# Expert coefficients by accumulating scatters from GpSimd in place of one-hot matmuls

## The reference, cut to what matters

```python
top_s, top_i = lax.top_k(sc, PEER_TOPK)               # 16 of 128 keys, in both halves
cand_s = top_s[:, :, 0, :, None] + top_s[:, :, 1, None, :]
best_s, best_pos = lax.top_k(cand_s, PEER_TOPK)       # 16 of the 256 sums
idx = jnp.take_along_axis(cand_i, best_pos, axis=-1)  # expert = 128 * first + second
g = jax.nn.softmax(best_s, axis=-1)
act = gelu(einsum('phkd,pd->phk', expert_u[idx], xb))
return einsum('phk,phkd->pd', g * act, expert_v[idx])
```

## Time and profile before

| | us |
|---|---|
| median of 3 runs | 2823.46 (2823.13 to 2825.11) |
| profiled execution, whole | 2823.46 |
| its span | 2821.4 |
| PE busy | 2656.9 (94%) |
| VectorE busy | 1571.4 (56%) |
| ScalarE busy | 921.2 (33%) |
| GpSimd busy | 524.8 (19%) |

### The profile page before, as it was taken

How to read it: one execution, slowest core, us unless ns; L and a number is a source line. 1 busy time by engine, 2 the same in 40 slices (tenths; PEclk the granted TensorE clock), 3 DMA queues, 4 the chain that set the end, 5 groups by cost and what they waited for, 6 DMA issues and landing times.

```text
span 2821.4 us, 30879 instructions
## 1 busy us (share of the span) xinstructions
PE 2656.9 (94%) x11948; PEld 2161.4 (77%) x11948; DVE 1571.4 (56%) x2920; ACT 921.2 (33%) x1344; POOL 524.8 (19%) x308
## 2 busy tenths in 40 slices
PE   3989987989899999999999999999999998999998
PEld 2777876767678888888888888888778766888887
DVE  7864598897976344433344456555363456533432
ACT  4433332323233232222322332334342443322221
POOL 5424332222222000000000000003330443111100
PEclk9988999989999999999999999999999799999999
DMA  6533234434446332333323545443234013222232
GB/s 243 201 112 120 88 122 131 161 111 150 149 148 210 132 127 99 126 126 119 127 95 129 189 177 216 154 153 128 70 109 143 4 60 105 91 96 97 90 96 84
DMA packets 146088, 358.97 MB, mean 127 GB/s; under 512 B 9652, under 2 KB 75316, under 8 KB 140696
## 3 DMA queue, kind: packets, MB, share of 16 engines
q1 hardware_dynamic: 141272, 304.31, 32.2%
q0 software_dynamic: 4672, 52.69, 4.8%
HBM read 298.44 MB, written 56.62 MB: 126 GB/s over the span
## 4 chain that ended last, share of the span: by engine, by line
PE 66%; DVE 4%; ACT 1%; issue 1%; DMA 1%; SPq 0%; POOL 0%; ACTq 0%; DVEq 0%; POOLq 0%
PE bank L448 20%; PE bank L444 20%; PE bank L445 20%; PE bank L572 1%; PE bank L724 1%; DVE one_hot L1533 1%; DVE prob_lo L1269 1%; PE bank L726 1%; PE bank L725 1%; PE bank_stat L470 0%; ACT prob_hi L1084 0%; PE bank L694 0%; DMA weight<-expert_coefs 0%; DVE one_hot L1528 0%; PE bank L710 0%
## 5 line engine op out<-in xcount | busy, mean ns | idle before, releaser
L444 PE MATMUL bank<-h_lo,weights_hi 128*128 128x512 f32 x2176 | 882.3, 405 | 36.8 <-ACT weights_hi L792 31.6
L445 PE MATMUL bank<-h_hi,weights_hi 128*128 128x512 f32 x2176 | 870.9, 400 | 0.0
L792 ACT ACTIVATE weights_hi<-weights_raw 128x1024 fp32r<-128x1024 f32 (+1 forms) x411 | 430.8, 1049 | 484.0 <-PE bank L448 382.9
L448 PE MATMUL bank<-h_hi,weights_lo 128*128 128x512 f32 x2176 | 556.4, 396 | 5.3 <-DVE weights_lo L1227 5.3
L444 PEld LDWEIGHTS bank<-h_lo,weights_hi 128*128 128x128 f32 x2176 | 417.9, 192 | 141.2 <-ACT weights_hi L792 31.9
L445 PEld LDWEIGHTS bank<-h_hi,weights_hi 128*128 128x128 f32 x2176 | 417.4, 192 | 98.0 <-issue 0.2
L448 PEld LDWEIGHTS bank<-h_hi,weights_lo 128*128 128x128 f32 x2176 | 410.2, 189 | 106.0 <-DVE weights_lo L1227 6.2
L1859 POOL TENSOR_TENSOR weights_lo<-weights_raw,weights_hi 128x1024 fp32r<-128x1024 f32 x128 | 320.5, 2507 | 625.3 <-ACT weights_hi L792 625.3
L1227 DVE TENSOR_TENSOR weights_lo<-weights_raw,weights_hi 128x1024 fp32r<-128x1024 f32 (+1 forms) x283 | 359.1, 1271 | 35.2 <-ACT weights_hi L792 34.6
L1421 DVE SCALAR_TENSOR_TENSOR residual<-bank,ada,residual 128x512 f32<-128x512 f32 x136 | 102.3, 752 | 406.1 <-PE bank L448 406.0
L444 PE MATMUL bank<-mixed_lo,weights_hi 128*128 128x512 f32 x768 | 299.0, 389 | 0.0
(11 more groups left out here) (353 smaller groups left out, 2633.7 us busy)
## 6 DMA issues: line engine op xcount, KB each, us to landing
weights_raw<-in_expert_u SPq DMA_DIRECT2D x128, 512.0 KB, 3.5
weights_raw<-in_expert_v SPq DMA_DIRECT2D x128, 512.0 KB, 3.3
expert_coefs<-stage SPq DMA_DIRECT2D x32, 1024.0 KB, 6.3
weight<-expert_coefs POOLq DMA_DIRECT2D x16, 2048.0 KB, 8.7
ada_raw<-in_w_ada SPq DMA_DIRECT2D x40, 512.0 KB, 4.5
hidden_store<-hidden SPq DMA_DIRECT2D x14, 1024.0 KB, 5.8
hidden<-hidden_store POOLq DMA_DIRECT2D x7, 2048.0 KB, 14.8
weights_raw<-in_w_ffn_gate SPq DMA_DIRECT2D x22, 512.0 KB, 3.2
```

The source lines that it names most:

```text
L444: M.matmul(bank[:], hi[:, c:c + P], m_lo[k], start=start and i == 0, stop=False)
L445: M.matmul(bank[:], hi[:, c:c + P], m_hi[k], start=False, stop=False)
L448: ins = M.matmul(bank[:], lo[:, c:c + P], m_hi[k], start=False, stop=stop and i == len(tiles) - 1)
L792: S.activation(w_hi[n % SPLIT][:, 0:w], w_raw[n % RAW][:, 0:w], ACT.Copy).then_inc(*hi_done.inc(n))
```

## The change

Places are now found by addresses. After a set of 128 tokens is routed, VectorE works out for each token and each of its 128 choices the address of the coefficient in DRAM (`place`, three instructions), and the softmax weights stand in `share`. GpSimd issues 4 x 8 x 16 = 512 indirect transfers: each takes one column of share (one word of each of 128 partitions) and adds it at the 128 addresses in `expert_coefs` (L1843 of the changed kernel). It waits after each 16 until they have landed, since two heads may choose one expert. Before that SyncE writes zeros over the 33.5 MB of expert_coefs, in 64 stores of 512 KB placed among the loads of w_in, w_out, w_q and the first 36 blocks of expert_u. The layout in DRAM has the 128 tokens of a set as its innermost dimension, so that a group's coefficients come in four loads with rows of 512 bytes, where before it was one load with 16 KB for each partition.

AHEAD is 15: 120 blocks of expert_u come in a row, with nothing between them on PE. 14 groups of activations are stored and read back instead of 7. Group 14 of expert_v comes after blocks 120 to 127, then groups 15 and 0 to 13. Low parts of expert_u from block 2 on are made by VectorE. The second pair of tiles (h_hi/h_lo) serves every other group from group 0 on; groups 14 and 15 both use mixed_hi/mixed_lo. The set of 128 tokens number tb is routed one step a block: blocks 0 to 9, 10 to 27, 28 to 45 and 46 to 63.

```diff
-AHEAD = 8
+AHEAD = 15
 KEPT = AHEAD - 1
-FIRST_U = 8
-PLACE_U = (16, 16, 15, 9)
+ROUTE_STEPS = HEADS + HEADS // 2 + 4 + 2
...
-POOL_LOW = set(range(0, BLOCK_AT["expert_u", AHEAD * GROUP - 1] + 2)) \
+POOL_LOW = set(range(0, BLOCK_AT["expert_u", 2])) \
...
-            second = N_GROUPS - 1 - KEPT
-            PAIR[g] = (i - second + 1) % 2 if i >= second else 0
+            PAIR[g] = (i + 1) % 2 if i else 0
...
+        ROUTED_AT = [[None] * HEADS + list(range(ROUTE_STEPS - HEADS))]
+        for tb in range(1, TB):
+            ROUTED_AT.append([ROUTED_AT[-1][-1] + 1 + n for n in range(ROUTE_STEPS)])
...
-            for j in range(FIRST_U):
+            for j in range(AHEAD * GROUP):
                 hidden_product(j)
-            turn_chosen(0)
-            for tb, n, first, end in PLACING:
-                for quad in range(first, end):
-                    place(tb, quad)
-                if n == PLACE_U[tb] - 1 and tb + 1 < TB:
-                    turn_chosen(tb + 1)
-                hidden_product(placed_block(tb, n))
...
+            for j in range(AHEAD * GROUP):
+                for tb in range(TB):
+                    if ROUTED_AT[tb][-2] == j:
+                        soften(tb)
                 hidden_gelu(j)
...
-                    if not (KEPT <= g < N_GROUPS - 2):
+                    if i:
                         mix_hi(i + 1, k)
...
+                if i == 0:
+                    for n in range(GROUP):
+                        mix_hi(1, n)
...
+                chain(V.scalar_tensor_tensor(place_f[:], chosen[:, 1, :], float(N_KEYS), chosen[:, 0, :], ALU.mult, ALU.add))
+                chain(V.tensor_scalar(place_f[:], place_f[:], float(P), col("token"), ALU.mult, ALU.add))
+                chain(V.tensor_scalar(place[:, tb, :], place_f[:], float(tb * N_KEYS * N_KEYS * P), None, ALU.add))
...
+            for j in range(AHEAD * GROUP):
+                for tb in range(TB):
+                    if j in ROUTED_AT[tb]:
+                        next(routers[tb])
+                split_lo(BLOCK_AT["expert_u", j] + 2)
...
+                if i == 0:
+                    for n in range(GROUP):
+                        late.append((MIX_ORDER[1], n))
+                        finish_mix()
...
-            for j in range(AHEAD * GROUP):
-                split_lo(BLOCK_AT["expert_u", j] + 2)
+            split_lo(BLOCK_AT["expert_u", 2])
-            G.wait_ge(*stage_stored[0][T // TOK - 2])
-            G.wait_ge(*stage_stored[1][T // TOK - 1])
+            for tb in range(TB):
+                G.wait_ge(*zeros_stored[tb][TB * TB - 1])
+                G.wait_ge(*dve["routed", tb])
+                for h in range(HEADS):
+                    if h:
+                        G.wait_ge(*scattered[tb, h - 1, TOPK - 1])
+                    for n in range(TOPK):
+                        c = h * TOPK + n
+                        G.indirect_dma_start(out=coefs[:], out_offset=bass.IndirectOffsetOnAxis(ap=place[:, tb, c:c + 1], axis=0),
+                                             in_=share[:, tb, c:c + 1], in_offset=None, compute_op=ALU.add) \
+                            .then_inc(*scattered.inc((tb, h, n)))
+            G.wait_ge(*scattered[TB - 1, HEADS - 1, TOPK - 1])
...
-                    G.dma_start(weight[g % 2][:].rearrange("p s j t -> p (s j t)"),
-                                coefs[g].rearrange("p s j t -> p (s j t)")).then_inc(*weight_landed[g % 2].inc(g))
+                    for tb in range(TB):
+                        G.dma_start(weight[g % 2][:, :, tb * P:tb * P + P],
+                                    coefs_of[tb, g * GROUP:g * GROUP + GROUP].rearrange("j p t -> p j t")) \
+                            .then_inc(*weight_landed[g % 2].inc((g, tb)))
...
+            def store_zeros():
+                if zeroed[0] < TB * TB * TB:
+                    tb, n = divmod(zeroed[0], TB * TB)
+                    Y.dma_start(coefs_of[tb, GROUP * n:GROUP * n + GROUP].rearrange("j p t -> p j t"),
+                                zeros[:].unsqueeze(1).broadcast_to([P, GROUP, P])).then_inc(*zeros_stored[tb].inc(n))
+                    zeroed[0] += 1
```

More of the change, by code:

```diff
@@ L202, in build @@
         keys_landed = signal("keys_landed", 16)
-        stage_stored = [signal(f"stage{i}_stored", 16) for i in range(2)]
+        zeros_stored = [signal(f"zeros{tb}_stored", 16) for tb in range(TB)]
+        scattered = signal("scattered", 16)
         hidden_stored = [signal(f"hidden{i}_stored", 16) for i in range(2)]
@@ L558, in hidden_product @@
                 product(("u", j), BLOCK_AT["expert_u", j], h_hi_tiles, h_lo_tiles)
[L560 to L564, removed]
-                ins.then_inc(*pe.inc(("turn", tb)))
-            def place(tb, quad):
-                bank = take(("place", tb, quad))
-                M.wait_ge(*dve["hot", tb, quad])
-                hot = one_hot[quad % N_HOT]
-                for t in range(4):
-                    ins = M.matmul(bank[:, t * P:(t + 1) * P], hot[:, 0, t, :], hot[:, 1, t, :], start=True, stop=True)
-                ins.then_inc(*pe.inc(("place", tb, quad)))
-            for j in range(FIRST_U):
-                hidden_product(j)
-            turn_chosen(0)
-            for tb, n, first, end in PLACING:
-                for quad in range(first, end):
-                    place(tb, quad)
-                if n == PLACE_U[tb] - 1 and tb + 1 < TB:
-                    turn_chosen(tb + 1)
-                hidden_product(placed_block(tb, n))
+            for j in range(AHEAD * GROUP):
+                hidden_product(j)
             for i, g in enumerate(MIX_ORDER):
@@ L1029, in mix_hi @@
                         S.wait_ge(*pe["v", pair_over, KD - 1])
-                    if PAIR[g] and not PAIR[MIX_ORDER[i - 1]] and i > 1:
+                    if PAIR[g] and not PAIR[MIX_ORDER[i - 1]]:
                         S.wait_ge(*pe["u", N_KEYS - 1])
@@ L2021, in save_hidden @@
                         .then_inc(*hidden_stored[g % 2].inc((g, n)))
-            def store_stage(tb, quad):
-                s = (tb * P + 4 * quad) // TOK
-                Y.wait_ge(*act["place", tb, quad])
-                Y.dma_start(coefs[:, :, s, :, :].rearrange("g p j t -> p g (j t)"),
-                            stage[s % 2][:].rearrange("p g j t -> p g (j t)")).then_inc(*stage_stored[s % 2].inc(s))
-            for j in range(FIRST_U):
+            for j in range(AHEAD * GROUP):
                 load_weights(BLOCK_AT["expert_u", j] + 5)
                 save_hidden(j)
-            for tb, n, first, end in PLACING:
-                for quad in range(first, end):
-                    if 4 * quad % TOK == TOK - 4:
-                        store_stage(tb, quad)
-                j = placed_block(tb, n)
-                load_weights(BLOCK_AT["expert_u", j] + 5)
-                save_hidden(j)
+                store_zeros()
             save_hidden(AHEAD * GROUP)
```

125 lines of the change are left out of this document (31 added, 94 removed).

## The result

The changed kernel took 3036.4 us (median of 4 runs, 3026.6 to 3041.3), the kernel before 2823.3 us beside it: a ratio of 1.075, 95% interval [1.073, 1.078]. The forecast was 2690 us and faster, with a chance of 0.63. It went the other way, and rival 2 (more than 1.46 us from one scatter to the next) is what happened. The forecast's wide range, 2600 to 3100 us, holds the time only because it took that rival in. The profiled execution has a span of 3036.7 us.

A forecast was written before the change was run, and what follows sets the result against it. PE bounds the kernel, then the scatters decide: 2821.4 - 217.0 (placing) - 4.8 (old stall) + 3.8 + 3.4 (tile order) = 2606.8, + 79.1 stall + 1.5 = 2687.4 us span; forecast 2690 us, range 2600 to 3100.

The forecast's parts named there:

- rival 2: GpSimd's scatters: one in more than 1.46 us makes the kernel slower than before; chance 0.35.
- I take 1.2 us an issue, about twice the plain one: GpSimd's time per scatter, against 0.54 us for a plain transfer; gave 21.8 us a round and a 79.1 us stall.
- break-even of 1.46: Microseconds per scatter issue on GpSimd, 26.0 us a round, at which the 214.6 us gain is used up.
- The landing: GpSimd's wait after each 16 scatters until they have landed: taken as 2.6 us, at the least 2.2.
- the case without overlap: The 16 scatters in flight don't overlap, each costing its landing of at least 2.2 us: 3118 us; chance 0.05.
- The sum around it: Whole kernel's span apart from the stall for coefficients: 2606.8 us, plus 1.5 us for matmuls at lower clock.
- VectorE's low parts and routing beside the first blocks: First expert_u blocks: low parts at 1.22 us each beside routing steps cost nothing, perhaps 1 us x 32 steps.
- The edge between groups 14 and 15: First two expert_v groups share mixed_hi, so group 15's tiles come late: +3.4 us on PE.
- rival 3: Coefficient loads in 512 B rows starve the expert_v stretch, 130 us over 13 groups: 2739 us; chance 0.04.
- rival 1: Scatters hidden behind the expert_u blocks, an issue of at most 1.05 us, no stall: 2609 us; chance 0.25.
- VectorE's port: Scatters may wait for VectorE's low parts at a shared SBUF port: 0.13 us each, 69 us more than 2690.
- The fixed cost of a transfer: About 2.0 us for each GpSimd transfer, mostly write confirmation; without overlap 1024 us of scatters, about 3016 us.

The follow-up runs named there:

- first head plain: Changed kernel, complete, but the first head's 16 transfers of each token set write instead of adding: 3011.3 us, ratio 1.067.
- two sets in turns: Changed kernel, complete, with scatter rounds of token sets 2 and 3 alternating, each waiting for the landing two rounds before: 3007.4 us, ratio 1.066.
- 64 rows: Changed kernel with all 512 adding scatters, each of 64 partitions instead of 128 (half of the tokens left out): 2989.6 us, ratio 1.060.
- 16 rows: Changed kernel with adding scatters of 16 partitions instead of 128 (seven eighths of the tokens left out): 2947.7 us, ratio 1.044.
- no add: Changed kernel with all 512 scatters writing their value instead of adding it (values wrong where routes meet): 2754.3 us, ratio 0.977.
- no add, 96 rows: Changed kernel with scatters that write without adding, of 96 partitions instead of 128: 2739.3 us in one run.
- four forms: Changed kernel with a quarter of the 512 transfers each indirect with add, indirect without, plain column with add, plain without: 2686.3 us, single run.
- half of the heads: Changed kernel with only heads 0 to 3 scattered, 256 transfers instead of 512: 2608.4 us, ratio 0.925.

## Why the prediction was wrong, step by step

**The failed step** is "I take 1.2 us an issue, about twice the plain one". Measured: 1.59 us in the mean and 0.30 to 0.35 us between two. Taken apart by the runs: 0.54 for the plain column, +0.42 for the indices, +0.59 for the add, +0.05 beside the other engines, and the gap. I had priced the indices, more or less, and at nothing both the add and the gap between two transfers; additions are named only in "That additions are lost would change values, not time". The cost of this step: (32.6 - 21.8) x 32 = 346 us, and 3036.4 - 2690 = 346. Of that the add is 512 x 0.588 = 301 us and the gap between two transfers 280.6 - 55.6 - 57.2 = 168 us (all idle time before the scatters, less the wait for the first routes and the landing waits). With the 24 us beside the other engines that is more than the whole; the 0.242 us by which 1.2 lay above an issue with indices and without add give 124 us back, and the landings, below, 26. The choice of the nearest row was the weak place: the earlier trace rows gave 0.54 and 2.40 us, the value was 0.54 doubled, and the middle of the two, 1.47, would have landed on the break-even of 1.46. What GpSimd does in the 1.55 us isn't shown; the packet records of the quiet stretch only show that no packet of a round's first scatter starts before its issue has ended, the first 0.57 us behind it.

**The landing** was near: 2.6 us were taken, 1.6 to 2.8 us measured in all but two of the waits (57 us in all). There are 28 waits and not 32, since the first head of a set waits for none. Transfers in flight overlap: one follows the other 0.30 us after its issue, where a landing is waited for at least 1.6 us. So the 0.05 for the case without overlap was rightly small, and it is chance that 3016 us, the prediction's estimate for that case from a fixed cost of 2.0 us, lies near the measured 3036 us.

**The sum around it held.** Take from each kernel's span its one long gap of PE: 3036.7 - 423.0 = 2613.7 for the changed one, and

| kernel | scatter, median us | coefficients' load from | gap of PE | span less gap |
|---|---|---|---|---|
| changed | 1.546 | 1419.7 | 423.0 | 2613.7 |
| first head plain | 1.555 / 0.957 | 1398.6 | 401.8 | 2607.9 |
| two sets in turns | 1.546 | 1395.2 | 397.9 | 2608.6 |
| 64 rows | 1.416 | 1378.2 | 382.3 | 2606.5 |
| 16 rows | 1.289 | 1333.3 | 337.0 | 2606.7 |
| no add | 0.958 | 1139.6 | 141.4 | 2617.0 |
| no add, 96 rows | 0.919 | 1125.7 | 131.3 | 2606.7 |
| four forms | mixed | 1075.7 | 69.9 | 2615.1 |
| half of the heads | 1.546 | 916.5 | none | 2604.6 |

The forecast's 2606.8 + 1.5 = 2608.3 us stands through all of it within 9 us, and the gap varies from 423 us to none. The rows "no add, 96 rows" and "four forms" are single runs. In every row with a gap the gap ends 12.1 to 12.5 us after the load's start (forecast 13 + 1.9).

**VectorE's low parts and routing beside the first blocks**, costed at nothing: PE busy 373.78 of 374 us. Right.

**The edge between groups 14 and 15** was given 3.4 us. PE's row there shows the first wait of 1.60 us, and the product took about 3 us more than its neighbours (its low-part matmuls stand 8.3 us behind the last ones, where 5.44 us is usual):

```profile
1514.86 0.47 PE L439 MATMUL bank<-mixed_lo,weights_hi 128*128 128x512 f32 x1 [1.60 <-DVE mixed_lo L1216]
```

**Coefficient loads that starve expert_v** (rival 3): PE busy 399.93 of 400 us from 1800 to 2200 us. It didn't happen. **Hidden** (rival 1) had the right time, 2609 us, for a queue half as long: 2608.4 us.

**VectorE's port.** While the other engines worked, rounds held 24.8 to 29.5 us of issue; in the idle stretch all held 24.8. The mean lies 0.05 us above the median here, 0.09 us for the form without add and 0.14 us with 16 rows. By the Trainium skill ("SBUF — State Buffer", SBUF: two separate sides) I had estimated 0.13 us, 69 us in all. The direction agrees, but the weight loads ran in the same stretch and no run parts the two. Whatever its cause, it explains (1.592 - 1.546) x 512 = 24 us of 346: GpSimd took its 1.55 us with VectorE idle too.

**The fixed cost of a transfer.** The Trainium skill ("DMA: Bandwidth & Descriptors", Anatomy of one DMA) puts most of some 2.0 us into the confirmation of the write and calls the generation of descriptors small. The landing waits, 1.6 to 2.8 us behind the last issue, are of the size of the 2.0 us; that most of it is confirmation isn't borne out in the quiet stretch, where the last packet starts about 1.1 us behind the issue and the next scatter 0.6 us after that. The second half doesn't hold for this form, if GpSimd's time is the writing of descriptors: 1.55 us for 128 words of 4 bytes, before any packet starts, and the measurement decides.

## What to carry to other kernels

Count a small GpSimd transfer (512 bytes here) by its issue, not by its bytes. With a list of indices and an add it holds the engine for about 1.55 us and the next comes after 1.85 us; with an eighth of the rows it is still 1.29 us. 512 of them are a millisecond, and worth it only as far as they end before the work that covers them. Where the trace has no row for an operation and the break-even lies between the two nearest ones, the sign is open, and each property of the new operation (indices, add, rows) needs a price of its own. When a cheap but slow path and a dear but quick one exist side by side, split the work at the point where the slow one just ends in time.

## What was not expected of the hardware

- An add in a transfer from GpSimd lengthens GpSimd's own instruction: by 0.36 us for a plain column of 128 elements, by 0.59 us with indices. GpSimd's queue in the changed kernel and in the one without add (packets, MB, share):

```profile
q0 software_dynamic: 86320, 67.67, 13.5%
```
```profile
q0 software_dynamic: 28976, 67.67, 7.8%
```

  These are (86320 - 28976) / 512 = 112 packets a transfer fewer. Yet little of the price is paid by the row: 1.546, 1.416 and 1.289 us with 128, 64 and 16 rows, 2.0 and 2.6 ns a row.
- Indirect transfers stand 0.30 us apart; plain ones follow each other at once.
- TensorE's granted clock was 0.50 (the 1.2 GHz level) in the idle stretch and 1.00 (2.4 GHz) from 1450 us on; the first eight matmuls after it took 3.78 us in place of 2.02.
- Indirect transfers without add on 64 partitions brought TensorE down to a matmul each 2.80 us, twice, where those on 96 and 128 partitions, and those with add on 128, 64 and 16, left it at full speed. Why is open.
